# A two-part transformer kernel on one core: the opening re-staged, with stacked tap weights, earlier sine arguments and half of the filter transforms moved

## The reference, cut to what matters

```python
a = rmsnorm(h, norm_mix[0])                      # h: 16 meta + 256 real tokens x 1024
for g, win in enumerate((2, 4, 8, 16)):          # pool_mixer, 256 channels a group
    pooled[g] = (cs - lag) / cnt - xg            # windowed mean of a, minus a
mix = einsum(pooled, w[g]) * scale
h = h + mix
h = h + (silu(x @ w_gate) * (x @ w_up)) @ w_down # x = rmsnorm(h, norm_ffn[0]): the gate stage

# hyena_filters, for the second block
hid = sin(fr * (z @ w1 + b1))                    # z: 256 x 33, w1: 33 x 64
hid = sin(fr * (hid @ w2 + b2))                  # w2: 64 x 64
taps = (hid @ w3).reshape(L, 2, 2, 512) * decay  # 2 directions, 2 orders
# long_conv_bidir: K = spectrum of [h_fwd, 0, h_bwd reversed], plus bias at lag 0
```

## Time and profile before

| | us |
|---|---|
| median of 3 runs | 1037.47 (1035.02 to 1037.66) |
| the profiled execution, its own time | 1035.64 |
| its span from first to last instruction | 1033.9 |
| PE busy in the span | 987.1 (95%) |
| DVE / ACT / POOL busy | 775.8 / 504.5 / 123.1 |

### The profile page before, as it was taken

The page is one execution under the profiler, slowest core; times in us unless marked ns, Lnnn a source line. Parts: engine busy times, 40 slices in busy tenths (PEclk is TensorE's granted clock), DMA queues, the critical chain, the costliest instruction groups (busy, mean ns, idle before and its releaser), DMA issues.

```text
span 1033.9 us, 20269 instructions
## 1 busy us (share of the span) xinstructions
PE 987.1 (95%) x7692; PEld 935.3 (90%) x7692; DVE 775.8 (75%) x1231; ACT 504.5 (49%) x740; POOL 123.1 (12%) x141
## 2 busy tenths in 40 slices
PE   5989999999999998999999999998989999999996
PEld 4379999999989988999999998987889999999995
DVE  6759888888766657999966775878575969876554
ACT  7345544344555544445544432575556565554441
POOL 4000000011100026400005401100000420000111
PEclk9689999999999999999999999999999999999999
DMA  7048777567743324656635633333333548654452
GB/s 233 1 165 301 250 271 260 200 240 259 244 142 124 123 77 151 226 218 245 249 130 187 212 133 118 123 143 128 108 133 123 209 172 294 241 175 165 168 185 79
DMA packets 38924, 186.26 MB, mean 180 GB/s; under 512 B 4984, under 2 KB 9625, under 8 KB 26010
## 3 DMA queue, kind: packets, MB, share of 16 engines
q1 hardware_dynamic: 38874, 185.57, 51.1%
HBM read 184.50 MB, written 1.05 MB: 179 GB/s over the span
## 4 chain that ended last, share of the span: by engine, by line
PE 77%; DVE 13%; ACT 4%; issue 3%; POOL 1%; DMA 1%; DVEq 0%; SPq 0%; ACTq 0%
PE ps L423 22%; PE ps L425 22%; PE ps L424 22%; DVE wl L364 4%; PE ps L1765 1%; ACT wh L358 1%; DVE dump L1262 1%; DVE dump L1268 1%; DMA stage<-in_w_k 1%; DVE xl L1217 1%; PE ps L1783 1%; PE ps L1809 1%; PE ps L1827 1%; PE ps L2033 1%; PE ps L1984 1%
## 5 line engine op out<-in xcount | busy, mean ns | idle before, releaser
L423 PE MATMUL ps<-xh,wh 128*128 128x256 f32 (+3 forms) x1808 | 524.7, 290 | 8.8 <-DVE xl L1217 3.6
L425 PE MATMUL ps<-xl,wh 128*128 128x256 f32 (+3 forms) x1808 | 517.3, 286 | 0.0
L424 PE MATMUL ps<-xh,wl 128*128 128x256 f32 (+3 forms) x1808 | 516.6, 286 | 0.0
L364 DVE TENSOR_TENSOR wl<-stage,wh 128x1024 fp32r<-128x1024 f32 (+2 forms) x320 | 363.2, 1145 | 125.5 <-ACT wh L358 123.6
L358 ACT ACTIVATE wh<-stage 128x1024 fp32r<-128x1024 f32 (+2 forms) x320 | 306.5, 968 | 175.8 <-PE ps L425 141.6
L423 PEld LDWEIGHTS ps<-xh,wh 128*128 128x128 f32 x1808 | 341.9, 189 | 15.1 <-issue 5.2
L424 PEld LDWEIGHTS ps<-xh,wl 128*128 128x128 f32 x1808 | 342.2, 189 | 2.8 <-issue 1.2
L425 PEld LDWEIGHTS ps<-xl,wh 128*128 128x128 f32 x1808 | 341.4, 189 | 1.4
L423 PE MATMUL ps<-gh,wh 128*128 128x256 f32 (+1 forms) x528 | 150.1, 284 | 2.9 <-DVE wl L364 1.5
L424 PE MATMUL ps<-gh,wl 128*128 128x256 f32 (+1 forms) x528 | 149.4, 283 | 0.0
L425 PE MATMUL ps<-gl,wh 128*128 128x256 f32 (+1 forms) x528 | 149.0, 282 | 0.0
(11 more groups left out here) (247 smaller groups left out, 783.1 us busy)
## 6 DMA issues: line engine op xcount, KB each, us to landing
stage<-in_w_gu SPq DMA_DIRECT2D x66, 1024.0 KB, 4.8
stage<-in_w_dn SPq DMA_DIRECT2D x48, 704.0 KB, 4.1
adaw<-in_w_ada SPq DMA_DIRECT2D x48, 512.0 KB, 5.0
stage<-in_w_gates SPq DMA_DIRECT2D x8, 1024.0 KB, 4.7
stage<-in_w_hy SPq DMA_DIRECT2D x6, 1024.0 KB, 4.8
stage<-in_w_q SPq DMA_DIRECT2D x8, 512.0 KB, 4.7
stage<-in_w_k SPq DMA_DIRECT2D x8, 512.0 KB, 5.1
stage<-in_w_v SPq DMA_DIRECT2D x8, 512.0 KB, 5.0
```

What stands on the lines that cost most here:

```text
L364: nc.vector.tensor_tensor(wl[:, b, w], stage[:, b, w], wh[:, b, w].bitcast(fp32), ALU.subtract).then_inc(split_lo, 1)
L423: nc.tensor.matmul(psum, wh[:, b, w], xhi, start=first and n == 0, stop=False)
L424: nc.tensor.matmul(psum, wl[:, b, w], xhi, start=False, stop=False)
L425: last = nc.tensor.matmul(psum, wh[:, b, w], xlo, start=False, stop=close and n == len(blocks) - 1)
```

## The change

In words:

- SP: the filter inputs are issued first, with `hpar` and `hw2` twice (into both halves of 128 rows), then h. hw3 is stored as two 64-row pieces, one direction above the other, ahead of the pool weights. cvec no longer waits for `k_read` and `stats`.
- Both directions' weights are stacked on 128 rows; `hid` gets 128 rows: kind 0 is (hid, hid), kind 1 is (hid, -hid), so one matmul over 128 rows yields the sum or the difference, and `wboth`, `hzero` and POOL's work are gone. The bias enters through a one-row matmul (L1766 after the change) on the last tap.
- Both sine arguments are computed by the DVE back to back, ahead of the pool's `xl`.
- The pool products use banks 4 to 7 in turn; tap products 0 to 3 come before them and 4 to 7 behind them.
- The window sums are taken over all remaining groups at once (8, 6, 4, 2 tiles), and `mixed` is gone.
- Transforms 0 to 3 and four of the gate's squares stay ahead of the gate stage; the other four squares and transforms 4 to 7 are issued after its first chunk (`rest_of_opening`).

The core of the diff:

```diff
@@ sync
+            for dst, src in ((zt, "zt"), (hw1, "hw1")):
+                sp.dma_start(dst[:, :], A[src]).then_inc(filter_in, 16)
+            for t in range(2):
+                sp.dma_start(hpar[HD * t:HD * t + HD, :], A["hpar"]).then_inc(filter_in, 16)
+                sp.dma_start(hw2[:, HD * t:HD * t + HD], A["hw2"]).then_inc(filter_in, 16)
             for j in range(2):
                 sp.dma_start(h[:, 4 * j:4 * j + 4, :], ...
-            for dst, src in ((zt, "zt"), (hw1, "hw1"), (hpar, "hpar"), (hw2, "hw2")):
-                sp.dma_start(dst[:, :], A[src]).then_inc(filter_in, 16)
...
-            sp.wait_ge(k_read, 8)
             sp.wait_ge(res, KD + RES0["pool"])
-            sp.wait_ge(stats, STAT["ffn0"])
             sp.dma_start(cvec[:, :, :], ...
@@ gpsimd
-            pool.wait_ge(z_arg, 1)
-            link(pool.tensor_scalar(hk[:, :], hx[:, :], 1.0 / (2 * math.pi), ROUNDER, ALU.mult, ALU.add))
...
-            pool.wait_ge(taps_in, 16 * 4)
-            for n, op in enumerate((ALU.add, ALU.subtract)):
-                pool.tensor_tensor(wboth[:, n, :], hw3[0:HD, 0:2 * HYW], hw3[0:HD, 2 * HYW:4 * HYW], op)\
-                    .then_inc(wboth_set, 1)
@@ scalar
+            act.preload_act_table(ACT.Sin)
+            for j in range(2):
+                act.wait_ge(h_in[j], 16)
+                for k in range(4 * j, 4 * j + 4):
+                    act.activation(squares0[:, k, :], h[:, k, :], ACT.Square).then_inc(sq0_ready, 1)
+                if j == 0:
+                    sine(0)
             act.wait_ge(param_in, 16)
             for k in range(KD):
                 pool_input_hi(k)
+                if k == 3:
+                    sine(1)
+                    act.wait_ge(hsign_set, 4)
+                    act.wait_ge(z_sin, 2)
+                    act.activation(hid[:, 1, :], hid[:, 0, :], ACT.Copy, scale=hsign[:, 0:1]).then_inc(hid_ready, 1)
+                    act.wait_ge(hid_ready, 1)
+                    act.activation(hid[HD:P, 0, TX - 1:TX], hid[HD:P, 0, TX - 1:TX], ACT.Copy, scale=0.0).then_inc(hid_ready, 1)
+            act.preload_act_table(ACT.Sqrt)
...
             root("ffn0", TM)
+            for i in range(4, 8):
+                spectrum_stored(i)
             act.wait_ge(cvec_in, 16)
@@ vector
+            def window_sums(i):
+                k0, shift = 2 * i, 1 << i
+                width = TM + META - 2 * shift + 1
+                src, dst = (y0, sums_a, sums_b, sums_a)[i], (sums_a, sums_b, sums_a, sums_b)[i]
+                link(dve.tensor_tensor(dst[:, k0:KD, 0:width], src[:, k0:KD, 0:width],
+                                       src[:, k0:KD, shift:shift + width], ALU.add))
...
+            link(dve.tensor_tensor(h[:, :, :], h[:, :, :], y0[:, :, 0:TM], ALU.subtract))
@@ tensor
+            def filter_taps(i):
+                o, t, kind = i // 4, i // 2 % 2, i % 2
+                holds_last = t == 1 and kind == 0
+                ins = pe.matmul(ps[i % 4][:, :], hid[:, kind, t:TX:2], hw3[:, o * HYW:(o + 1) * HYW], start=True,
+                                stop=not holds_last)
+                if holds_last:
+                    ins = pe.matmul(ps[i % 4][:, :], hlast[:, :], hbias[:, o * HYW:(o + 1) * HYW], start=False, stop=True)
+                ins.then_inc(f_out, 1)
+
+            def filter_spectrum(i):
+                o, part, f = i // 4, i // 2 % 2, i % 2
+                t = PARITY(part, f)
+                if i >= 3:
+                    pe.wait_ge(k_read, i - 2)
+                pe.matmul(ps[SPECTRUM_BANK(i)][:, :], (cosf, sinf)[part][:, t, :], gboth[o][:, part, t, :], start=True,
+                          stop=True).then_inc(k_out, 1)
...
+            pe.wait_ge(pool_read, KD)
+            for i in range(4):
+                filter_spectrum(i)
+            for k in range(4):
+                gate_squares(k)
+
+            def rest_of_opening():
+                for k in range(4, KD):
+                    gate_squares(k)
+                pe.wait_ge(f_read, 8)
+                for i in range(4, 8):
+                    filter_spectrum(i)
-            two_tiles("gu0", wide(0, TM), TM, (k_read, (2, 4)), (nlo, IN0["pool"] + 1))
+            two_tiles("gu0", wide(0, TM), TM, (f_read, (6, 8)), (nlo, IN0["pool"] + 1), rest_of_opening)
```

More of the change, by code:

```diff
@@ L109, in PARITY, with POOL_BANK, SPECTRUM_BANK @@
     return 1 - f if part == 0 else f
+def POOL_BANK(m):
+    return 4 + m % 4
+def SPECTRUM_BANK(i):
+    return 4 + i % 3
 def MIX_BANK(m):
@@ L507, in build @@
         taps_in = sem("tap_weights_in")
+        decay_in = sem("decay_in")
         pool_hi = sem("pool_input_hi")
@@ L1257, in _ @@
             lo_part("gu0", PAIR0["gu0"], 0, 1)
+            for i in range(6, 8):
+                taps(i)
             def modulate_tile(n, q, b, ctx_col=None):
@@ L1754, in _ @@
                 pe.wait_ge(split_lo, g + 1)
                 pe.wait_ge(pool_lo, 2 * g + 2)
-                last = products(ps[m][:, 0:TM], b, (2 * j, 2 * j + 1), wide(ALT, TM, 2 * g, 2 * g + 2))
+                last = products(ps[POOL_BANK(m)][:, 0:TM], b, (2 * j, 2 * j + 1), wide(ALT, TM, 2 * g, 2 * g + 2))
                 if m % 2:
                     last.then_inc(used, 1)
-            pe.wait_ge(wboth_set, 2)
-            pe.wait_ge(z_sin, 2)
-            for i in range(8):
-                o, t, kind = i // 4, i // 2 % 2, i % 2
-                pe.wait_ge(pool_read, i + 1)
-                pe.matmul(ps[i][:, :], hid[:, 1, t:TX:2], wboth[:, kind, o * HYW:(o + 1) * HYW],
-                          start=True, stop=True).then_inc(f_out, 1)
@@ L1767, in _ @@
-            pe.wait_ge(const_in, 16 * 7)
-            pe.wait_ge(hzero_set, 1)
-            pe.wait_ge(hzero_hid, 1)
-            for i in range(8):
-                o, part, f = i // 4, i // 2 % 2, i % 2
-                pe.wait_ge(f_read, 4 * o + 4)
-                t, shared = PARITY(part, f), part == 0 and f == 0
-                ins = pe.matmul(ps[i][:, :], (cosf, sinf)[part][:, t, :], gboth[:, o, part, t, :], start=True,
-                                stop=not shared)
-                if shared:
-                    ins = pe.matmul(ps[i][:, :], hzero[:, :], hw3[:, (2 + o) * HYW:(3 + o) * HYW], start=False, stop=True)
-                ins.then_inc(k_out, 1)
@@ L1780, in _ @@
[L1780 to L1785 removed]
+            pe.wait_ge(f_read, 4)
+            for i in range(4, 8):
+                filter_taps(i)
+            pe.wait_ge(const_in, 16 * 7)
+            pe.wait_ge(pool_read, KD)
```

198 lines of the change are left out of this document (92 added, 106 removed).

## The result

The changed kernel takes **1030.07 us** (median of 6 runs, 1027.17 to 1031.2) against 1037.57 for the kernel before in the same jobs (6 runs, 1035.02 to 1039.81): ratio 0.9927, 95% interval 0.9908 to 0.9946, so 7.5 us faster. The forecast was 1028.8. The profiled execution took 1027.17 (before 1035.64), 8.5 less.

What follows compares the result with a forecast made beforehand. PE bounds it, busy 987.1 of 1033.9 us. Summing the new path puts chunk 3 at 67.1 instead of 75.9: 8.8, less 0.1 for rounding, takes the 1037.47 median to 1028.8 us; range 1025.5 to 1033.5.

Steps and rivals of the forecast that it cites:

- What bounds it: Whole kernel: PE bounds; the gain is how much earlier chunk 3 starts, 67.1 instead of 75.9, 8.8 us.
- Filters, sines, pool: Opening: filters land at 5.7, second sine starts at 14.35, first squares end at 17.5, pool's `wl` at 22.2.
- late filters: Opening, rival: small transfers land at 7.1, shifting the path 1.4; gain 7.3, 1030.2 us; chance 0.08.
- Stacked rows and the clock: Opening's taps on PE: stacking on 128 rows costs nothing; a tap takes 0.86 us at the high clock.
- The sum: Step times added along the new path: first gate product 47.9, chunk 3 at 67.1, gain 8.8 us.
- the rival of an opening at 1.2 GHz: PE from 11.4 to 30, rival: clock stays low, `y0` 9.9 us later; 1040.2 us; chance 0.06.
- Mixing: DVE after `y0` at 30.2: long window sums, subtraction, updates of h ending at 46.0, first gate product at 47.9.
- First chunk: Gate stage's chunk 1 on PE: 6.05 us at the high clock, from 47.9 to 53.95.
- low clock into the gate stage: Chunk 1, rival: clock not risen by then, costing 2.3 to 3 us; gain 6.1, 1031.4 us; chance 0.18.
- Behind chunk 1: Moved squares and transforms, norm and tables: chunk 2 at 60.0 to 66.1, PE waits 1.0, chunk 3 at 67.1.
- The other rivals: Late filters 0.08; table drain 1032.9 us, 0.02; work only moved, wait recurring, 1035.8, 0.08; opening at 1.2 GHz 0.06.

Runs made afterwards that it cites:

- h-first run: The changed kernel with the two transfers of h issued ahead of the six small filter inputs again; 1029.06 us, ratio 0.9921.
- after: The changed kernel itself, with the whole change, measured against the kernel before; 1030.07 us, ratio 0.9927.
- 64-row run: The changed kernel with the eight tap products on the first 64 rows only, second direction left out; 1029.09 us, ratio 0.9925.
- one-table: The changed kernel without ACT's second load of the Silu table in the gate stage's first round; 1027.04 us, ratio 0.9897.
- GpSimd-beside: The changed kernel with two unused 64x1024 additions on GpSimd beside the DVE's mixing; 1030.9 us, ratio 0.9946.
- by-group run: The changed kernel with window sums, subtraction and updates of h taken group by group again; 1031.29 us, ratio 0.9950.
- all-ahead run: The changed kernel with all eight squares and all eight transforms ahead of the gate stage again; 1028.97 us, ratio 0.9908.
- 128-row run: The kernel before with its taps' matmuls on 128 rows, the added 64 rows being zeros; 1032.21 us, ratio 0.9952.

## Why the prediction was right, and where a term was off

**What bounds it: right.** The gain is how much earlier chunk 3 starts, and from there the two kernels run alike: 7.1 at chunk 3, 6.9 at 755. The median fell by 7.5.

**Filters, sines, pool: right,** within 0.4 us at each step but the first squares (and h, whose first square came at 8.44 and not 7.75, off the path). These ended at 16.5, not 17.5: 5.12 us for sixteen records are fewer slow ones than assumed. (The windows list the clock as 1.00 there, though PE starts 6 records in 12:14 and 10 in 14:16; in the first microseconds the records tell it, not that column.) Nothing waited for it, as `hid` came at 15.67. The price named for late filters, 1.4, is the 1.5 that the h-first run shows.

**Stacked rows and the clock: right in size, unproven then.** The sum took the taps at 0.86 because squares had raised the clock; the old taps' 14 us at 0.50 stood against it, and carried the rival of an opening at 1.2 GHz. The rows now bear on it: 128-row taps raise the clock behind the same pause where 64-row ones stayed at 0.50 for 14 us in three traces, and it fell once, without a gap, behind four 64-row taps, though not behind the next four. The Trainium skill (TensorE: Matmul & The Clock Gate, section "HAM oscillation") speaks of idle gaps that return PE to the low clock; the falls behind pauses agree, and the 14 us of 64-row taps show that a PE without gaps isn't enough here.

**Mixing: right.** Sums 2.55, 1.93, 1.32, 0.72, subtraction 2.42 against 2.54, 1.93, 1.32, 0.73, 2.4; the four updates of h end at 36.2, 39.1, 42.3 and 46.0, all as forecast. The slope from operations of 574 and 1024 elements held up to 2296.

**First chunk: the term that was mis-sized.** The sum has it at 6.05 us, 47.9 to 53.95; it took 7.6, to 55.6. This is the place and the effect of the rival "low clock into the gate stage", but not its way: it had a clock that hadn't risen yet, and here it rose at about 44.5 (0.98 in 44.5:45) and fell again at 48. The rival's pause was 1.2 us; it was 2.2, as the squares had run at the high clock in part and ended sooner. Its price was put at 2.3 to 3 and was 1.6, as the clock was back by 52, some 3 us into the chunk, where 4.5 to 6 were assumed. Which of the two comes was decided by less than the forecast could tell. In after and in the 64-row run the clock came up within the last squares (they took 2.69 and 3.07), PE then paused 2.22 and 2.13, and it fell. In the one-table, h-first and GpSimd-beside runs it came up at their end or in the pause (squares 3.83, 3.58, 3.83), the pause was 1.07 to 1.32, and it stayed up through chunk 1. The length of the pause alone doesn't decide it: the by-group run kept its clock through 2.20.

**Behind chunk 1: right.** From its end to chunk 3 are 13.4 us against 13.15 in the forecast (53.95 to 67.1), with the wait ahead of chunk 3 at 0.90 instead of 1.0, and it doesn't recur. But the forecast booked this as the price of a gain, and the all-ahead run shows there was no gain in it: without the move chunk 3 comes 0.5 sooner. The forecast of the whole didn't need it, since it summed the new path from start to end.

**The other rivals** didn't come: the filters landed at 5.64, no table load was followed by a drain, PE was busy without a gap from 80 to 180 us, and `y0` was done at 30.05, not later than 38.9.

**The sum.** 8.8, less 1.7 for chunk 1 and 0.3 for what is behind it, plus 0.2 because chunk 3 of before started at 76.14 and not 75.9, is 7.1 at chunk 3. The profiled execution came out at 1027.17 against 1026.9 only since 1.6 us of another low clock, at 766, fell into the profile of before and not of after. Of the parts, run alone on the kernel before, the wait for GpSimd is worth 3.1 and 128 rows 4.0 at chunk 3; taken out of the changed kernel, the long sums are worth 2.6, 128 rows 0.4, and GpSimd's absence 3.0 at the first gate product. They don't add up: in the 128-row run one wait visibly hid the next.

## What to carry to other kernels

Sum the new path from its start to the point where the work is the same again, and test each moved piece by where the engine would have stood idle otherwise: a norm's sums belong ahead of the stage that needs the norm if the engine waits there anyway, and its root, reciprocal and table loads then lie beside matmuls. Price each stretch of PE at both clock levels, and where a pause of a few us stands ahead of a long stage, fill it or expect either. Compare landmarks near the change, not only totals: here 1.6 us of the profiled difference were far behind it.
